# Forgetting attention of a hybrid decoder layer: prompt attention placed inside the paged one, separate slots for key and value pages, eight pages to a score round

## The reference, cut to what matters

```
cum = jnp.cumsum(logf, axis=1)
# prompt, per block of 128 queries, 16 heads of 64
logits = einsum('bqhd,bkhd->bhqk', qb, k) * FOX_SCALE + cum_q[..., None] - cum_k[..., None, :]
logits = where(q_pos >= k_pos, logits, NEG_INF)
o = einsum('bhqk,bkhd->bqhd', softmax(logits), v)
# streams
k_past = k_pool[page_table]; v_past = v_pool[page_table]; lf_past = lf_pool[page_table]
suffix = lax.cumsum(lf_all, axis=1, reverse=True) - lf_all
logits = einsum('bqhd,bkhd->bhqk', q, k_all) * FOX_SCALE + suffix[:, :, None, :] - suffix[:, :, p_len:, None]
o = einsum('bhqk,bkhd->bqhd', softmax(where(mask, logits, NEG_INF)), v_all)
```

## Time and profile before

| | us |
|---|---|
| median of three runs | 3816.0 (3813.73 to 3816.32) |
| profiled execution | 3816.24 |
| its span | 3814.6 |
| PE busy | 3390.1 (89%) |
| DVE busy | 1572.4 (41%) |
| ACT busy | 1059.2 (28%) |
| POOL busy | 240.9 (6%) |

### The profile page before, as it was taken

The page is one execution under the profiler, slowest core; times in us unless marked ns, Lnnn a source line. Parts: engine busy times, 40 slices in busy tenths (PEclk is TensorE's granted clock), DMA queues, the critical chain, the costliest instruction groups (busy, mean ns, idle before and its releaser), DMA issues.

```text
span 3814.6 us, 64314 instructions
## 1 busy us (share of the span) xinstructions
PE 3390.1 (89%) x26621; PEld 3033.2 (80%) x26621; DVE 1572.4 (41%) x2273; ACT 1059.2 (28%) x1437; POOL 240.9 (6%) x279
## 2 busy tenths in 40 slices
PE   7998899998999999988999866279999799889997
PEld 6897799988944466667999754179999698779997
DVE  2324544333134411226442379854432432464423
ACT  3301322222022244433222234342222320232222
POOL 0000000004300000000000057200000000000000
PEclk9996899999966699998999988689999899789998
DMA  3113232313110199962223211023232110422331
GB/s 93 56 34 111 72 88 87 92 53 84 38 48 1 56 377 393 392 246 68 86 87 91 55 44 44 12 67 88 87 91 76 56 51 27 124 70 85 88 91 46
DMA packets 465044, 367.67 MB, mean 96 GB/s; under 512 B 16329, under 2 KB 429438, under 8 KB 464924
## 3 DMA queue, kind: packets, MB, share of 16 engines
q1 hardware_dynamic: 449808, 348.72, 28.4%
q10 hardware_dynamic: 11020, 16.22, 1.2%
q0 software_dynamic: 4096, 1.06, 0.3%
HBM read 348.68 MB, written 17.26 MB: 96 GB/s over the span
## 4 chain that ended last, share of the span: by engine, by line
PE 82%; DVE 9%; issue 4%; ACT 3%; DVEq 0%; POOL 0%; DMA 0%; ACTq 0%; SPq 0%; POOLq 0%
PE acc L668 54%; PE acc L649 6%; PE acc L1005 3%; DVE big L1244 3%; PE acc L952 2%; PE acc L940 2%; PE acc L942 2%; PE acc L975 2%; PE acc L1044 2%; PE acc L864 2%; PE acc L852 1%; DVE rstd L1274 1%; PE acc L728 1%; ACT mix L2176 1%; PE acc L962 1%
## 5 line engine op out<-in xcount | busy, mean ns | idle before, releaser
L668 PE MATMUL acc<-h_hi,wsp 128*128 128x272 f32 x5632 | 943.3, 289 | 65.9 <-DVE h_lo L1530 65.9
L1266 DVE TENSOR_TENSOR wsp<-ring,wsp 128x1024 fp32r<-128x1024 f32 (+1 forms) x320 | 416.9, 1306 | 1164.2 <-ACT wsp L1893 1164.2
L668 PEld LDWEIGHTS acc<-h_hi,wsp 128*128 128x128 f32 x5632 | 797.9, 190 | 68.7 <-issue 68.4
L1893 ACT ACTIVATE wsp<-ring 128x1024 fp32r<-128x1024 f32 (+1 forms) x320 | 358.4, 1124 | 1297.6 <-PE acc L668 1294.5
L668 PE MATMUL acc<-h_lo,wsp 128*128 128x272 f32 x3328 | 690.0, 289 | 0.0
L668 PEld LDWEIGHTS acc<-h_lo,wsp 128*128 128x128 f32 x3328 | 527.3, 190 | 0.0
L668 PE MATMUL acc<-g_hi,wsp 128*128 128x272 f32 x2816 | 473.5, 290 | 24.0 <-DVE g_lo L1525 24.0
L668 PEld LDWEIGHTS acc<-g_hi,wsp 128*128 128x128 f32 x2816 | 400.9, 190 | 24.9 <-issue 24.9
L668 PE MATMUL acc<-i_hi,wsp 128*128 128x272 f32 x1536 | 265.1, 295 | 37.2 <-DVE i_lo L1294 32.4
L668 PE MATMUL acc<-g_lo,wsp 128*128 128x272 f32 x1408 | 292.4, 289 | 0.0
L668 PEld LDWEIGHTS acc<-i_hi,wsp 128*128 128x128 f32 x1536 | 224.8, 195 | 39.6 <-issue 35.5
(11 more groups left out here) (287 smaller groups left out, 3442.0 us busy)
## 6 DMA issues: line engine op xcount, KB each, us to landing
ring<-in_ffn_w SPq DMA_DIRECT2D x176, 512.0 KB, 3.8
mix<-in_cache_fox_k SPq DMA_DIRECT2D x96, 512.0 KB, 9.5
mix<-in_cache_fox_v SPq DMA_DIRECT2D x96, 512.0 KB, 10.2
ring<-in_ffn_w SPq DMA_DIRECT2D x64, 704.0 KB, 4.5
big<-in_cache_fox_k SPq DMA_DIRECT2D x32, 512.0 KB, 8.5
big<-in_cache_fox_v SPq DMA_DIRECT2D x32, 512.0 KB, 13.1
ring<-in_conv_w SPq DMA_DIRECT2D x24, 512.0 KB, 3.9
ring<-in_gla_wr SPq DMA_DIRECT2D x16, 512.0 KB, 3.7
```

What stands on the lines that cost most here:

```text
L668: last = pe.matmul(acc[:, bank + h, 0:HALF], wsp[:, s, w, k * P:(k + 1) * P], rhs[:, k0 + k, h * HALF:(h + 1) * HALF], start=start and k = ...
L1266: dve.tensor_tensor(wsp[:, s, 1, 0:tiles * P], ring[:, slot, 0:tiles * P], wsp[:, s, 0, 0:tiles * P], ALU.subtract).then_inc(wlo_done, 1)
L1893: act.activation(wsp[:, slot % SPLITS, 0, 0:tiles * P], ring[:, slot, 0:tiles * P], ACT.Copy)\
```

## The change

The two attentions become one program of 37 steps (STEPS), written out without a loop. Step s does the following, on PE in this order: it turns the output of the last prompt pair (turn_output); from step 5 on, transposes the probabilities of four value pages (turn, v = s - 5); in every even step from 2 to 32, a score round over eight key pages (sample_scores); in steps 0 to 31, the scores of a pair of prompt items (scores_of_pair); two value pages (weigh, part 0); the transposes of the pair (turn_pair); the other two value pages (part 1); the pair's values (values_of_pair).

- Key pages are no longer turned by PE and copied by ACT. DVE turns each in 32x32 blocks in one instruction (turn_pages, L1635, 128x1024), into the single buffer kT of eight pages.
- A score round is four matmuls for the biases, one per 32-row quadrant (L1028), and 128 matmuls of 32 rows by 32 columns of the array with 256 moving columns (L1046), on all 16 row and column positions; row quadrant a writes bank a. ACT copies all four banks out in one instruction (L2162) and DVE takes the maximum half a stream at a time (L1648).
- The biases are worked out for all streams beforehand (L1184 and before it), added on DVE, and sent by 20 small DMAs from ACT's queue into their quadrants (L2129, L2133). DVE waits for all of them before its fifth key page.
- The prompt pair: two items of the same q side by side, mask added by a matmul (L989), scores, transposes and values all in banks 6 and 7 in turn; the division moves onto the 64 output columns; the output is turned and goes into the queries' columns of `big` instead of `hT`.
- Keys have four page slots (three in `mix`, one in `ring`), values four (in `ring`). SP issues key page n, then value page n - 16; each waits until its slot's previous page was used.
- The prompt's key rows, the forget gate and a copy of the streams' queries and keys into every quadrant (L2111, L2113) now come ahead of the value projection, and the first three key pages are loaded during it.
- The output weights are loaded when the last value page was used.

The diff, cut to what the steps above need:

```diff
+        def k_page(n):
+            r = n % K_SLOTS
+            return part(F4 + r * D, D) if r < K_MIX else ring_flat[:, 0:D]
+        def v_page(n):
+            r = n % V_SLOTS + 1
+            return ring_flat[:, r * D:(r + 1) * D]
+        V_BEHIND = NPAGES
+        PAIR_STEPS = FH * PT // 2
+        LAG = NPAGES // GR + 1
+        STEPS = PAGES // GR + LAG
...
-                sp.wait_ge(nat_out, 16 * (PT + 5))
-                sp.wait_ge(pv_out, PAIRS)
+                    if n >= slots:
+                        sp.wait_ge(freed, n - slots + 1)
+                    sp.dma_start(slot, cache[0, ds(numbers[kind][n % NPAGES], 1)].rearrange("a p h d -> p (a h d)"))\
+                      .then_inc(landed, 16)
...
+                for n in range(K_MIX, PAGES + V_BEHIND):
+                    if n < PAGES:
+                        load_page("k", n)
+                    if n >= V_BEHIND:
+                        load_page("v", n - V_BEHIND)
+                sp.wait_ge(v_used, DB * NPAGES)
                 load_out(w_view(fox_wo[0]))
...
+            def sample_scores(G):
...
+                pe.wait_ge(turned, KG * (G + 1))
+                for c in range(GH4):
+                    for f in range(2):
+                        cell = 2 * c + f
+                        for a in range(GR):
+                            quad = slice(32 * a, 32 * (a + 1))
+                            for j in range(GR):
+                                h = GH4 * j + c
+                                at = (2 * h + f) * 32
+                                last = pe.matmul(acc[32 * j:32 * (j + 1), a, 0:NK], qz[quad, b % 2, h, f, :],
+                                                 kT[quad, :, at:at + 32], start=False, stop=(cell == 2 * GH4 - 1),
+                                                 skip_group_check=True, tile_position=(32 * a, 32 * j))
...
+            def turn(v):
...
+                if u == 0:
+                    pe.wait_ge(zexp_done, b + 1)
+                    pe.wait_ge(orow_done, b)
...
+                elif u == 1:
+                    pe.wait_ge(ot_out, b)
...
+            def attention():
+                for s in range(STEPS):
+                    v, pair = s - LAG, s < PAIR_STEPS
+                    if 0 < s <= PAIR_STEPS:
+                        turn_output(s - 1)
+                    if v >= 0:
+                        turn(v)
+                    if s % 2 == 0 and 2 <= s <= 2 * DB * HALVES:
+                        sample_scores(s // 2 - 1)
+                    if pair:
+                        scores_of_pair(s)
+                    if v >= 0:
+                        weigh(v, 0)
+                    if pair:
+                        turn_pair(s)
+                    if v > 0 and v % GR == 0:
+                        output(v // GR - 1)
+                    if v >= 0:
+                        weigh(v, 1)
+                    if pair:
+                        values_of_pair(s)
...
+            def turn_pages(G, pages):
+                for g in pages:
+                    n = G * KG + g
+                    dve.wait_ge(ksc_full, G)
+                    dve.wait_ge(k_in[n % K_SLOTS], 16 * (n // K_SLOTS + 1))
+                    dve.transpose(kT[:, g, :], k_page(n)).then_inc(turned, 1)
...
+                    elif more:
+                        turn_pages(G, (4, 5))
+                    if pair:
+                        for x in range(2):
+                            n = item(2 * s + x)[2]
+                            dve.wait_ge(sc_full, 2 * s + x + 1)
+                            dve.tensor_reduce(nmax[:, x:x + 1], acc[:, 6 + x, 0:n], AX.X, ALU.max, negate=True)\
+                               .then_inc(pmax_done, 1)
...
+                    if more:
+                        turn_pages(G, (6, 7) if s % 2 else (0, 1, 2, 3))
```

More of the change, by code:

```diff
@@ new lines, in output @@
+            def output(b):
+                pe.wait_ge(orow_done, b + 1)
+                pe.wait_ge(pt_out, min(GR * (b + 1) + 1, DB * GR))
+                for q in range(2):
+                    last = pe.transpose(acc[:, 4, q * P:(q + 1) * P], orow[:, q * P:(q + 1) * P], ident[:])
+                last.then_inc(ot_full, 1)
+            def attention():
[19 more added lines that the diff above has]
+                        values_of_pair(s)
@@ L1110, in fox @@
                     t.use(bank)
+                h_ready()
+                pe.wait_ge(vec_in, VEC_FOX)
+                pe.wait_ge(acc_out[0], t.out[0])
+                for k in range(KD):
+                    for h in range(2):
+                        last = pe.matmul(acc[0:FH, h, 0:HALF], wg1_sb[:, k, :], hT[:, k, h * HALF:(h + 1) * HALF],
+                                         start=(k == 0), stop=(k == KD - 1))
+                last.then_inc(acc_full[0], 1)
+                t.use(0)
+                for b in (2, 4):
+                    pe.wait_ge(acc_out[b], t.out[b])
@@ L1139, in fox @@
-                for c in range(LFN // 512):
-                    bank = 2 * (c % 4)
-                    pe.wait_ge(acc_out[bank], t.out[bank])
-                    pe.matmul(acc[:, bank, :], ones[:], later.rearrange("p b g h -> p (b g h)")[:, c * 512:(c + 1) * 512],
-                              start=True, stop=True).then_inc(acc_full[bank], 1)
-                    t.use(bank)
-                wait_banks()
-                sample_attention()
-                wait_banks()
+                    last = pe.transpose(acc[0:n, 4, tt * FH:(tt + 1) * FH], logf[:, tt * P:tt * P + n], ident[0:FH, 0:FH])
@@ new lines, in fox @@
+                last.then_inc(acc_full[4], 1)
+                t.use(4)
+                pe.wait_ge(lf_in, 16 * DB * NPAGES)
+                for g in range(NPAGES):
+                    last = pe.matmul(acc[:, g // GR, (g % GR) * P:(g % GR + 1) * P], lf[:, g].rearrange("p b h -> p (b h)"),
+                                     strict[:], start=True, stop=True, skip_group_check=True)
+                last.then_inc(suf_full, 1)
+                pe.wait_ge(lnm_done, 1)
+                lnew = lnm.rearrange("p b h -> p (b h)")
@@ new lines, in fox @@
+                pe.matmul(acc[:, 5, 0:NPAGES], lnew, ones[0:NS, 0:NPAGES], start=True, stop=False, skip_group_check=True)
+                pe.matmul(acc[:, 5, NPAGES:NPAGES + DS], lnew, gt4, start=False, stop=False, skip_group_check=True)
+                for g in range(1, NPAGES):
+                    last = pe.matmul(acc[:, 5, 0:g], lf[:, g].rearrange("p b h -> p (b h)"), ones[:, 0:g], start=False,
+                                     stop=(g == NPAGES - 1), skip_group_check=True)
+                last.then_inc(sums_full, 1)
```

870 lines of the change are left out of this document (394 added, 476 removed).

## The result

| | before | after |
|---|---|---|
| median of the runs, us | 3816.16 (3813.73 to 3816.32) | 3941.6 (3934.86 to 3945.63) |
| profiled execution, its span | 3816.24, 3814.6 | 3939.4, 3937.8 |
| mean granted clock | 0.905 | 0.876 |
| first matmul of the output projection | 1684.47 | 1807.09 |

The ratio is 1.0327 (95% interval 1.0312 to 1.0341): slower, by 125.4 us where 76 were forecast and 3892 stood as the time. The value is inside the range (3745 to 4010) and inside the likeliest case's own (3840 to 3980). In the two profiled executions the output projection starts 122.6 us later and the spans differ by 123.2, so all of it lies ahead of the output projection, where the forecast put it.

What follows compares the result with a forecast made beforehand. Prompt attention was taken as PE-bound at the low clock, paged attention as DMA-bound beside busy PE. 1093 + 52 + 567 + 39 = 1751, 72 beyond 1679.4, plus 4 for output weights: 3816.2 + 76 = 3892 us; range 3745 to 4010.

Steps and rivals of the forecast that it cites:

- likeliest case: Whole kernel: pairs of steps take 38.4 to 48 us, time 3840 to 3980 us; chance 0.61.
- the forecast's chain: Odd step: key page 5 issued only after a value slot comes free, both transfers 5.2 us, turn 1.15, then DVE's maximum.
- The prologue: Up to the first prompt maximum: value projection ends at 1066, then 27 us of preparation, ending at 1093.
- The 13.5 pairs: 27 steps from step 5 on, as odd and even pairs of 42 us each: 567 us.
- 3.0 a pair: Output row behind the fourth key page's turn 4.2 us, output copies 2.5: 6.7 in 6 of 13.5 pairs.
- the eighth key page: Issued after the odd step's third value page, in kT 4.0 us later, needed by PE at 2.2: 1.8 us wait.
- The tail: Last five steps, without prompt pairs: 15 us for last round and exponential, then four times 6, together 39.
- The score round: 256 instructions of 32x32 tiles on PE: 6.1 us if row quadrants run at once, 14.8 as far end.
- that rival (4031): Row tiles don't overlap: 14.8 us for 6.1 in 16 score rounds, 139 more, 4031; chance 0.10.
- the rival of 2.3: DVE turns a key page in 2.3 us instead of 1.15: about 3 us more a pair, 3935; inside the forecast's range.
- The clock: Low PE clock expected in odd steps, +6 us, half of that in even ones; stage's granted clock near 0.75.
- The rival that steps pack: Clock up, row quadrants and halves overlapping: 32.8 us a pair, 3752; decided from 36.5 downwards; chance 0.23.

Runs made afterwards that it cites:

- e1: Changed kernel with value page n - 20 instead of n - 16 issued behind key page n on SP: 3802.6 us, ratio 0.9957 to the kernel before.
- e7: Changed kernel with value page n - 18 instead of n - 16 issued behind key page n on SP: 3783.2 us, ratio 0.9908 to the kernel before.
- e8: Changed kernel with value pages issued from GpSimd's queue, key pages still from SP: 3796.7 us, ratio 0.9947 to the kernel before.
- e2: Changed kernel with the output row and output copies ahead of the same step's page turns on DVE: 3864.7 us, ratio 1.0121 to the kernel before.
- e4: Changed kernel with 248 of 256 page transfers and their waits left out, the first four pages of each kind reused: 3683.7 us, ratio 0.9643.
- e5: Changed kernel with four unused 128 by 512 matmuls on PE in each odd step, where it waits for the exponentials: 3930.5 us, ratio 1.0296.
- e10: Changed kernel with keys 18 ahead of values on SP; on DVE output row and copies ahead of turns, all turns behind the pair's maximum: 3750.0 us, ratio 0.9828.
- e9: Changed kernel with value pages from GpSimd's queue; on DVE output row, output copies and the pair's maximum ahead of page turns: 3776.1 us, ratio 0.9892.

## Why the prediction was right, and where its sizes were off

**The mechanism.** Slower, because SP's order and four slots a kind put a transfer's latency into every second step: e1 and e7 change only this order, e8 takes the values out of it, and they take 139 to 158 us off, and the timeline has the forecast's chain link by link. The rows named beforehand are there: the maximum behind a page of `cache_fox_k`, PE idle for about 8 us (6.74 at L998 in the timeline; 6.7 to 7.4 in pairs with an output row, 8.9 to 10.7 in the others), 189 GB/s where under 250 stood.

**The sum**, step by step in the profiled executions, makes 46.6 us more than 76:

- *The prologue*, forecast to end at 1093, ended at 1102.8: +9.8. Six of it are ahead of the value projection, which ended at 1072 and not at 1066. Behind it the 20 small transfers begin at 1084.22, 12.2 us after that end and not 10.1 (+2.1), their issue takes 12.8 us and not 10 (+2.8), and the last has landed 1.2 us after it and not 2.5 (-1.3). DVE's fifth turn waits for it. From the timeline of the changed kernel:

```profile
1084.22 10.25 ACTq L2129 DMA_DIRECT2D mix<-yT  x16
...
1094.51 2.53 ACTq L2133 DMA_DIRECT2D big<-big  x4
...
1098.22 3.50 DVE L1635 STREAM_TRANSPOSE kT<-mix 128x1024 f32<-128x1024 f32 x3 [9.92 <-DMA big<-big]
...
1102.77 0.45 DVE L1661 TENSOR_REDUCE big<-acc 128x1 f32<-128x128 f32 x2
```

- *Steps 0 to 4*: from 1102.8 to 1158.0, 55 us for 52.
- *The 13.5 pairs*: from 1158.0 to 1757.5, 599.5 us for 567, which is 44.4 a pair and not 42: +32.5. This is the term that was mis-sized, chiefly in one place, "3.0 a pair" for the output row and its copies. Pairs come in two lengths. By the round starts

```profile
1264.48 1.24 PE L1028 MATMUL acc<-mix,big 32*128 32x256 f32 x8
...
1300.24 1.24 PE L1028 MATMUL acc<-mix,big 32*128 32x256 f32 x8
...
1352.76 1.24 PE L1028 MATMUL acc<-mix,big 32*128 32x256 f32 x8
```

  one without an output row takes 35.8 us and one with it 52.5. Over the stage the seven short ones have a mean of 36.8, where the forecast's numbers give 39 (42 less 3.0), and the six long ones 53.9, where they give 45.7 (39 and 6.7). Six times 8.2 more and 7.5 times 2.2 less are 33. I had let PE wait 4.2 us for the row, the length of the turns ahead of it, as if their pages were there. PE waited 47.6 / 6 = 7.9, since these turns were waiting for pages of their own; and 24.1 / 6 = 4.0 for the copies, not 2.5. The same fault that I had found for pages 4 and 5 also held for pages 0 to 3, and I did not carry it over. These two waits make 5.2 of the 8.2 us; the other 3.0 are about what the low clock behind them can take, by e2 up to 4.7 us of PE's work in such a pair. e2 shows the size of the whole: 77 us. The other way went the eighth key page: 1.8 us a pair in the forecast, and 6.2 us in four waits in all, 0.5 a pair.
- *The tail*, 40 us for 39, and *the output weights*: 9.5 us from the last value page to the first matmul, against 5.1 before, so +4.4 for +4.

**Unit prices.** The score round, the largest unknown, took 5.6 us in the stage's fastest case (1760.73 to 1766.33, 256 instructions, 0.47 us of it idle), for 6.1 with 14.8 as the far end:

```profile
1760.73 4.65 PE L1046 MATMUL acc<-kT,mix 32*32 32x256 f32 x225 [1.14 <-DVE kT L1635]
1765.85 0.72 PE L1046 MATMUL acc<-kT,mix 32*32 32x256 f32 x31 [0.47 <-issue]
1766.33 0.90 PE L1054 MATMUL acc<-mix 32*32 32x32 f32 x64
```

Most rounds were slower: from the third to the last 5.6 to 7.7 us, a mean of 6.7 at the stage's clock of 0.71. In e4, at 0.92, the mean is 5.6 (5.0 to 6.4). So row tiles run beside each other, and that rival (4031) is out. For the high clock the 5.6 us that the prediction worked out from the Trainium skill (TensorE: Matmul & The Clock Gate, Measured speedup vs the span model) was the better figure, and e4's mean agrees with it; in the changed kernel's own stage 6.1 was nearer. The biases took 0.71 to 1.24 for 1.2. DVE's turn has a mean of

```profile
L1635 DVE STREAM_TRANSPOSE kT<-mix 128x1024 f32<-128x1024 f32 x90 | 111.6, 1244 | 163.2 <-DMA mix<-in_cache_fox_k 162.8 <-issue 0.3
```

1.24 us for 1.15, which rules out the rival of 2.3. The pair's scores came out cheaper: two heads on different row halves overlap, 0.70 us for four instructions of 256 columns at the high clock and 1.23 at the low one. One after the other the four would take 0.9 to 1.06 at the high clock: 1.06 by the earlier trace rows, 0.9 by e5, where eight instructions of 512 columns took 3.7. That, and the eighth page, are reasons why short pairs are shorter than forecast.

**The clock.** The stage had 0.71 (0.69 from 1175 to 1620) for 0.75. I had given it 9.6 us a pair (from 38.4 to 48) and taken 6 back for scores that overlap. PE's busy time for the same instructions, the thirteen pairs from the third round to the last, shows what it costs PE (us, from the profiled executions):

| kernel | thirteen pairs | PE busy | clock |
|---|---|---|---|
| after | 581.5 | 372.1 | 0.71 |
| e1 | 447.9 | 373.2 | 0.76 |
| e7 | 440.7 | 359.6 | 0.79 |
| e10 | 399.4 | 335.7 | 0.86 |
| e4 | 349.8 | 311.8 | 0.92 |

From after to e4 that is 60 us, 4.6 a pair, of PE's time: a smaller term than the 9.6. How much of the 4.6 is on the path, no run shows. e5 raised the clock by 0.08 and won 0.6 us a pair, with the page waits left in place.

**The rival that steps pack** needed under 36.5 us a pair. The forecast's 38.4 us at the high clock hold 10.0 of waits for pages and turns (5.2, 1.8 and 3.0), so the engines' own chain is 28.4 in it, and 22.8 in the rival's 32.8. e4 has 26.7, at a clock of 0.92: between the two, nearer the forecast. What speaks against the rival was written beside it, the latency that stays in the odd step, and that decided. With the order mended, e10 gives 3750, where that rival stood (3752); that the two agree is in part chance, since it takes 30.2 us a pair to get there and not 32.8.

**What stays open.** How much of PE's slower work at the low clock is on the path: every run that takes page waits away raises the clock too. And whether one queue with keys two ahead is truly better than two queues: the medians say so (e7 under e8 by 13 us, e10 under e9 by 26), the profiled executions only for the second pair (e8's was 6 us the faster), and what GpSimd's own issuing costs was not taken apart.

## What to carry to other kernels

Where one queue issues two kinds of transfer, each with a wait for its own slot, write down for every transfer which wait stands ahead of it in the queue and when that ends; a shift of two in the order was worth 158 us here, and a shift of four 139. When a wait is found in such a chain, go through every other consumer of the same resource with it: the output row's stop was the same fault, seen once and not looked for again. And look at the order before making any instruction faster: with PE, DVE and DMA all below two thirds busy, changes of order alone, on SP and on DVE, took 192 us off this kernel (after to e10).

## What the runs showed of the hardware that was not expected

- 256 matmuls on 32x32 tiles of the array with 256 moving columns, all fp32, ran in 5.6 us, 22 ns from start to start (the changed kernel's last round; e4's mean is the same at a clock of 0.92), though one takes 0.49 us in the mean of all 4096.
- Two matmuls of 64 rows on different row halves overlap as well: four instructions of 256 columns in 0.70 us, where e5's eight of 512 columns, on all rows and so one after the other, took 3.70.
- Useless matmuls in PE's gaps raised the granted clock from 0.69 to 0.77 and gave back 11 us of 3942.
- The same PE instructions kept PE busy for 372 us at a granted clock of 0.71, 336 at 0.86 and 312 at 0.92.
- A 512 KB page issued by GpSimd lands as fast as one by SP: in e8 medians of 6.9 us for values, and 6.8 to 8.2 for the keys on SP. The issue itself took 0.53 us on GpSimd and 0.33 on SP.
